# Two modulation items of an attention step put one behind the other, behind the second block of values

## The reference

```python
mod = (jax.nn.silu(cond) @ lp['w_ada'] + lp['b_ada'])[:, None, :]
sh1, sc1, g1, sh2, sc2, g2 = jnp.split(mod, 6, axis=-1)
h = rmsnorm(x, lp['norm1']) * (1 + sc1) + sh1
proj = h @ lp['w_in']
...
y = jnp.concatenate([y_a, y_b, y_c, y_d], axis=-1) @ lp['w_out']
x = x + g1 * y
```

## Time and profile before

| what | value |
|---|---|
| median of 3 runs | 1819.02 us (1817.84 to 1819.35) |
| the profiled execution, its own time | 1815.29 us |
| its span | 1813.5 us |
| PE busy, share of the span | 1678.7 us (93%) |
| PEld busy | 1516.1 us (84%) |
| DVE, ACT, POOL busy | 1037.9, 603.1, 532.2 us |
| chain that ended last | PE 61%, issue 20%, POOL 9%, ACT 4%, DVE 3%, DMA 1% |

### The profile page before, as it was taken

The page is one execution under the profiler, slowest core; times in us unless marked ns, Lnnn a source line. Parts: engine busy times, 40 slices in busy tenths (PEclk is TensorE's granted clock), DMA queues, the critical chain, the costliest instruction groups (busy, mean ns, idle before and its releaser), DMA issues.

```text
span 1813.5 us, 29689 instructions
## 1 busy us (share of the span) xinstructions
PE 1678.7 (93%) x11702; PEld 1516.1 (84%) x11702; DVE 1037.9 (57%) x1647; ACT 603.1 (33%) x1109; POOL 532.2 (29%) x297
## 2 busy tenths in 40 slices
PE   6999998988999999998789999899799999999966
PEld 4887555888999999998768955569699999999966
DVE  4284445237666666666534644532676666666655
ACT  3423444325222232222242244542432222222223
POOL 1354010222333334333125500113133333333320
PEclk8999999999999999999889999999899999999988
DMA  8323540121222222222343154202122222222211
GB/s 314 103 70 113 163 140 13 47 59 47 71 80 71 69 81 69 75 77 93 134 136 93 59 164 147 71 25 74 31 71 73 79 77 74 78 73 69 70 35 59
DMA packets 147729, 156.17 MB, mean 86 GB/s; under 512 B 8200, under 2 KB 118324, under 8 KB 147636
## 3 DMA queue, kind: packets, MB, share of 16 engines
q1 hardware_dynamic: 147636, 154.87, 27.5%
HBM read 151.54 MB, written 3.31 MB: 85 GB/s over the span
## 4 chain that ended last, share of the span: by engine, by line
PE 61%; issue 20%; POOL 9%; ACT 4%; DVE 3%; DMA 1%; POOLq 0%; ACTq 0%; SPq 0%; DVEq 0%
PE PS L1142 56%; POOL W_lo L839 8%; PE PS L1146 5%; ACT HF L913 1%; ACT PT L885 1%; POOL SS L855 1%; DMA AS<-in_w_ada_dram 1%; ACT PR L1019 1%; DVE X L1678 0%; DMA BS_N<-in_w_ada_dram 0%; ACT W_hi L885 0%; ACT H_hi L885 0%; DMA XIN<-in_x_sample_dram 0%; DVE H_lo L1652 0%; ACT PMM L885 0%
## 5 line engine op out<-in xcount | busy, mean ns | idle before, releaser
L839 POOL TENSOR_TENSOR W_lo<-RW,W_hi 128x1024 fp32r<-128x1024 f32 (+1 forms) x184 | 471.8, 2569 | 989.5 <-ACT W_hi L885 989.5
L1142 PE MATMUL PS<-H_hi,W_hi 128*128 128x384 f32 x1856 | 578.6, 312 | 18.9 <-DVE H_lo L1652 7.9
L1142 PE MATMUL PS<-H_hi,W_lo 128*128 128x384 f32 x1856 | 579.0, 312 | 0.0
L1142 PE MATMUL PS<-H_lo,W_hi 128*128 128x384 f32 x1856 | 578.7, 312 | 0.0
L1142 PEld LDWEIGHTS PS<-H_hi,W_hi 128*128 128x128 f32 x1856 | 354.2, 191 | 20.6 <-issue 13.5
L1142 PEld LDWEIGHTS PS<-H_lo,W_hi 128*128 128x128 f32 x1856 | 352.8, 190 | 0.1
L1142 PEld LDWEIGHTS PS<-H_hi,W_lo 128*128 128x128 f32 x1856 | 352.7, 190 | 0.0
L1142 PE MATMUL PS<-G_hi,W_hi 128*128 128x384 f32 x704 | 220.4, 313 | 34.0 <-DVE G_lo L1925 34.0
L885 ACT ACTIVATE W_hi<-RW 128x1024 fp32r<-128x1024 f32 (+1 forms) x184 | 191.2, 1046 | 128.1 <-PE PS L1142 128.1
L1142 PE MATMUL PS<-G_lo,W_hi 128*128 128x384 f32 x704 | 219.6, 312 | 0.0
L1142 PE MATMUL PS<-G_hi,W_lo 128*128 128x384 f32 x704 | 219.3, 311 | 0.0
(11 more groups left out here) (188 smaller groups left out, 1942.7 us busy)
## 6 DMA issues: line engine op xcount, KB each, us to landing
RW<-in_w_up_dram SPq DMA_DIRECT2D x88, 512.0 KB, 3.7
RW<-in_w_ada_dram SPq DMA_DIRECT2D x64, 512.0 KB, 4.0
RW<-in_w_down_dram SPq DMA_DIRECT2D x44, 512.0 KB, 3.6
RW<-in_w_in_dram SPq DMA_DIRECT2D x28, 512.0 KB, 3.7
AS<-in_w_ada_dram SPq DMA_DIRECT2D x16, 512.0 KB, 11.5
RW<-in_w_out_dram SPq DMA_DIRECT2D x32, 128.0 KB, 2.8
RW<-in_w_out_dram SPq DMA_DIRECT2D x8, 512.0 KB, 3.4
BS_N<-in_w_ada_dram SPq DMA_DIRECT2D x8, 512.0 KB, 7.7
```

Of the source, the lines that this page charges most:

```text
L839: nc.gpsimd.tensor_tensor(W_lo[:, slot, 0:width], RW[:, raw, 0:width], W_hi[:, slot, 0:width].bitcast(F32), ALU.subtract).then_inc(w_lo, 1)
L1142: return nc.tensor.matmul(out, lhsT, rhs, start=start, stop=stop, skip_group_check=True)
```

## The change

Both items of a step, with whatever goes along with them (MOVE, AT), are put behind the second values, one behind the other. Nothing else in the list moves, and the amount of work is the same.

```diff
-        order += [("S", s)] + ([("YA_HI",)] if n == 0 else []) + ptr[:2] + [("MAX", s)] + next(ada, []) + val[:1] + ptr[2:] + [("EXP", s, 0)]
-        order += x[:half] + next(ada, []) + val[1:2] + x[half:] + val[2:]
+        order += [("S", s)] + ([("YA_HI",)] if n == 0 else []) + ptr[:2] + [("MAX", s)] + val[:1] + ptr[2:] + [("EXP", s, 0)]
+        order += x[:half] + val[1:2] + next(ada, []) + next(ada, []) + x[half:] + val[2:]
```

## The result

| | median | runs | ratio to before, 95% |
|---|---|---|---|
| before | 1818.43 us | 1817.74 to 1819.35 | |
| after | 1830.58 us | 1826.5 to 1831.34 | 1.0062 [1.0044, 1.0079] |
| after, measured once more (e7) | 1828.24 us | 1824.99 to 1831.24 | 1.0058 [1.0045, 1.0072] |

The kernel became slower, by 12.2 us in the first measurement and by 9.6 us in the second, against 1818.63 us of before beside it. 8 us were forecast. The profiled execution of after took 1831.34 us with a span of 1829.5 us; e7's took 1825.73 us with a span of 1823.9.

What follows compares the result with a forecast made beforehand. PE's instruction order was taken to bound the steps with modulation items. Steps 1 to 8 add 2.17 us and 9 to 16 1.85, 8.0 in two layers: 1819.0 + 8.0 = 1827.0 us, range 1821 to 1836.

Steps and rivals of the forecast that it cites:

- The first item leaves the hole: In front of the first values: of the item's 0.57 us, 0.32 us stay as a wait for ACT's copy.
- Ordinary steps: Steps 2, 6, 11, 12 and 15: 0.32 us of wait less 0.14 of gain, +0.18 us each.
- steps 10 and 13: Steps with two fills and a larger hole: 0.54 us of wait less 0.14 of gain, +0.40 us each.
- step 9: First values already wait 1.10 us for ACT and don't move; the second item adds +0.43 us.
- The pair: Two items side by side cost 1.00 in place of 1.14 us; gain 0.14 us, bounds zero to 0.14.
- MOVE: ACT's MOVE, in front of the second exponentials, comes later and delays next scores: step 3 +0.77 us, step 7 +0.55.
- Step 12: Counted among the steps of the ordinary kind, at +0.18 us.
- Step 16: A lone AT waiting 0.49 us in the hole leaves it and joins the transposes: -0.20 us.
- Steps 1 and 5: Nothing transposed behind second values, so items split second and third values: +0.33 us, but +0.16 in step 5.
- Loads: Items free two ring slots 0.43 us apart, costed at nothing; rival: some 16 steps wait 1 us, 1843 us, 4%.
- The clock: Half-clock stretches, 1.3 us each, bounds -1.3 to +2.6; rival: clock falls in many steps, 1840 us, 6%.
- Covered after all: Rival, not slower: exponentials' chain sets the steps, new waits fill PE's standing time; 1816 to 1820 us, 13%.

Runs made afterwards that it cites:

- e7: The same kernel as after, measured once more with six runs; 1828.24 us, ratio 1.0058.
- e5: After, with the first block of values in steps 1 to 15 taking a constant tile, so it waits for no copy; 1817.73 us in one run.
- e1: Before, with both items of a step put side by side in front of the first values; 1817.10 us, ratio 0.9987.
- e8: Before, with the pair in front of first values except steps 10, 14, 15, MOVE behind second exponentials, output DMAs later; 1814.41 us, ratio 0.9983.
- e4: After, with MOVE put behind the second half of the exponentials in ACT's order; 1825.41 us, ratio 1.0039.
- e2: After, with the pair moved from behind to in front of the second values; 1829.41 us, ratio 1.0060.

## Why the prediction was right

**The first item leaves the hole: right.** Ordinary steps came out at +0.18 or +0.19 (2, 6, 11 and 15 in e7; 0.18 forecast), steps 10 and 13 at +0.40 and step 9 at +0.43 as forecast, step 14 at +0.28 as forecast. e5 shows the wait itself at 0.32 us, at 0.54 in steps 10 and 13, and at 0.99 in step 9, of which 0.57 is new. The prediction says of steps 10 and 13 that their hole is larger because they have two fills. But steps 11, 12 and 15 have two as well; what differs is that the second one has two blocks, so that in before PE is done with the transposes after 0.80 us (step 10) and not 1.02 (step 2).

**The pair: right.** 1.00 us to the next group, and 0.14 us of gain in e1 and e8 where nothing else changes.

*The Trainium skill, "TensorEngine Tiling (Array Packing)", section "Key Properties", says that a change of tiling mode drains the engine; this case's rows agree in so far as a pair, which saves one change, costs 0.14 us less. That the engine drains they don't show.*

**MOVE: right.** Step 3 +0.77 and step 7 +0.58, forecast 0.77 and 0.55. e4 takes them back to -0.21 and +0.19.

**Terms that were mis-sized,** all small. Step 12 got -0.01 in place of +0.18. I had put it with the ordinary steps, but an AT goes along in it as in steps 4 and 8, and it now stands next to a group of the same tile, 128*128. Step 16 got -0.01 in place of -0.20: the first values come 0.36 us earlier, as meant, but AT costs 0.26 us in its new place, where I had set 0.16, and the transposes start 0.08 us later behind the scores. Steps 1 and 5 got +0.40 and +0.24 in place of 0.33 and 0.16, since their first values wait 0.55 to 0.56 us instead of 0.49. Together the terms make 4.27 us for steps 0 to 15, forecast 4.2. That the sum comes so close is in part luck: step 12 is 0.19 us less than forecast, and steps 1, 5, 7, 8 and 4 together 0.25 more.

**Loads: costed at nothing, with a price past 5.2 us.** Two loads of step 1 in layer 1 of after took 5.52 and 6.33 us. Step 2 lost 0.30 us to the first of them, and nothing waited for the other. An item that waits for its load was on the prediction's list of signs against it; it is the rival's mechanism at a fiftieth of its price, and e7 has none. In e1 and e2, where the pair stands earlier, it is more.

**The clock: right in kind, short in size.** A stretch at half clock came to steps 13 and 14 of both layers in the profile of after, some 1.2 us each, as the bounds had it; before has one in step 14 of layer 0. That the clock might be lower in the long stages behind the attentions, by 3 us each, was not in the sum; all other stages were to stay the same. By the estimate above the clock makes 2.7 of the 10.2 us between the mean spans.

*The Trainium skill, "TensorE: Matmul & The Clock Gate", section "A second HAM failure mode: psum-queue depth-cycling", tells of a kernel whose clock falls again and again as PE idles briefly between groups of matmuls. Apart from the stretch in steps 13 and 14, no run bears it out for these steps: e7's layer 1 waits in every step from 1 on, and its granted clock is 1.00 over steps 0 to 15.*

**Covered after all: wrong, as forecast.** Where the chain of exponentials does set the next scores, in step 5, e5 brings 0.24 us and not the whole wait. In step 9 it brings 0.99 us of the 1.14 by which the values start earlier; elsewhere the wait passes through in full.

## What to carry to other kernels

Before moving work out of a spot, ask which copy it covers there, and read that copy's release from a step where nothing stands in the spot: the difference is the price of the move. Put short pieces of one tile shape side by side, but inside a hole that must be there anyway. On each engine that walks a fixed list, keep work that waits for a late producer behind the work that others wait for.

## What the runs showed of the hardware

Two slabs of 512 KB requested 0.43 us apart land after about 4.0 and 4.8 us (in steps 2 and 3 of layer 0 of e7 3.99 and 4.79, 3.86 and 4.66). The second takes some 0.8 us longer than the first. That is not the pair's alone: in step 3 of before, with 1.53 us between them, two loads took 4.03 and 4.83 us; in step 10, with 3.50 us between them, 3.80 and 3.53. A load close behind another needs more lead.

The same kernel's stage behind an attention lasts 718.9 or 721.6 us by the clock it is granted (0.66 and 1.00, or 0.58 and 0.83, in the stretches shown). A difference of 2.7 us there between two single profiles says nothing of the edit.
